# A two-block transformer kernel: the end of the FFN by tile and half, the output stored tile by tile, and the first weight piece of six stages split in halves by ScalarE and VectorE

## The reference

```
for i in range(2):
    h  = modulate_2(rms_norm_2(x, g_norm1[i]), sh1, sc1)
    p  = h @ w_in[i]                       # "proj": 7 column blocks of w_in
    ...                                    # neighbourhood, gating and latent attention
    mix = merge_branches(y_na, y_gm, y_mla, gate_logits, na_w_o, gm_w_o, mla_w_o, w_out)
    x_new = x + gt1 * mix                  # "merge": gates (from h and w_in) times y @ w_o
    x_new = x_new + gt2 * squared_relu_mlp(modulate_2(rms_norm_2(x_new, g_norm2[i]), sh2, sc2),
                                           ffn_w1[i], ffn_w2[i])
return x
```

## Time and profile before

| | us |
|---|---|
| median of 3 runs | 3921.87 |
| lowest and highest of them | 3921.0, 3926.0 |
| time of the profiled execution | 3927.83 |
| its span | 3926.0 |
| TensorE busy in it | 3386.4 (86%) |
| ScalarE, VectorE, GpSimd busy | 1140.5, 1595.3, 648.5 |

### The profile page before, as it was taken

One profiled execution on the slowest core, in us unless ns is written; L12 is line 12 of the kernel. 1 busy time (PEld: TensorE's weight loads), 2 busy tenths in 40 slices (PEclk: granted clock), 3 DMA queues, 4 the chain that ended last, 5 costly groups with the idle time before them and its releaser, 6 DMA issues. The chain is left out here.

```text
span 3926.0 us, 41596 instructions
## 1 busy us (share of the span) xinstructions
PE 3386.4 (86%) x16307; PEld 2397.5 (61%) x16307; DVE 1595.3 (41%) x2658; ACT 1140.5 (29%) x1931; POOL 648.5 (17%) x468
## 2 busy tenths in 40 slices
PE   4999774887756998888999799999599798988998
PEld 2666662222225865456887688888485456867886
DVE  3336642000024635552333533333565553344444
ACT  3113521111123235442221322211235443323221
POOL 2000001000004233123220100000445124400000
PEclk8999786899988989899999899999799999999999
DMA  6883045999976110002112312111611003233332
GB/s 260 330 318 140 2 144 163 429 428 428 428 317 189 61 25 11 9 36 83 65 43 86 118 65 65 55 64 43 200 61 34 9 36 105 86 131 105 97 97 75
DMA packets 162441, 534.02 MB, mean 136 GB/s; under 512 B 12252, under 2 KB 67412, under 8 KB 139228
## 3 DMA queue, kind: packets, MB, share of 16 engines
q1 hardware_dynamic: 139148, 401.22, 27.7%
q0 software_dynamic: 16640, 92.08, 6.7%
q10 hardware_dynamic: 6480, 38.34, 2.5%
HBM read 488.84 MB, written 42.78 MB: 135 GB/s over the span
## 5 line engine op out<-in xcount | busy, mean ns | idle before, releaser
L2926 PE MATMUL ps<-hT_hi,w_hi 128*128 128x512 f32 (+1 forms) x768 | 276.0, 359 | 28.0 <-DVE w_lo L2980 28.0
L2926 PE MATMUL ps<-hT_hi,w_lo 128*128 128x512 f32 (+1 forms) x768 | 275.9, 359 | 0.0
L2926 PE MATMUL ps<-hT_lo,w_hi 128*128 128x512 f32 (+1 forms) x768 | 275.4, 359 | 0.0
L1992 PE MATMUL ps<-wp_hi,hT_hi 128*128 128x512 f32 (+2 forms) x608 | 222.2, 365 | 37.3 <-POOL wp_lo L1971 37.3
L2932 PE MATMUL ps<-w_hi,h_lo 128*128 128x512 f32 x640 | 253.7, 396 | 0.0
L2932 PE MATMUL ps<-w_hi,h_hi 128*128 128x512 f32 x640 | 253.7, 396 | 0.0
L2932 PE MATMUL ps<-w_lo,h_hi 128*128 128x512 f32 x640 | 253.6, 396 | 0.0
L2205 PE MATMUL ps<-Z 64*128 64x256 f32 (+3 forms) x576 | 204.3, 552 | 27.9 <-DVE small L2347 11.6
L2645 POOL TENSOR_TENSOR mr_lo<-ring,wm_hi 128x2048 fp32r<-128x2048 f32 x36 | 171.0, 4763 | 312.8 <-ACT wm_hi L2637 312.7
L1994 PE MATMUL ps<-wp_hi,hm_lo 128*128 128x512 f32 (+2 forms) x608 | 220.0, 362 | 0.0
L2949 ACT ACTIVATE w_hi<-ring 128x2048 fp32r<-128x2048 f32 x64 | 122.0, 1909 | 336.6 <-PE ps L2932 326.8
(11 more groups left out here) (458 smaller groups left out, 6684.6 us busy)
## 6 DMA issues: line engine op xcount, KB each, us to landing
pj<-in_expert_w_up_dram SPq DMA_DIRECT2D x32, 2048.0 KB, 18.3
pj<-in_expert_w_down_dram SPq DMA_DIRECT2D x32, 2048.0 KB, 19.7
ring<-in_expert_w_gate_dram SPq DMA_DIRECT2D x32, 2048.0 KB, 16.0
ring<-in_ffn_w_dram SPq DMA_DIRECT2D x64, 1024.0 KB, 5.2
ring<-in_w_in_dram SPq DMA_DIRECT2D x58, 1024.0 KB, 5.4
Z<-in_w_mod_dram POOLq DMA_DIRECT2D x24, 2048.0 KB, 8.1
Z<-in_w_ada_dram POOLq DMA_DIRECT2D x8, 2048.0 KB, 9.4
ring<-in_w_out_dram SPq DMA_DIRECT2D x12, 1024.0 KB, 10.0
```

Of the source, the lines that this page charges most:

```text
L1992: nc.tensor.matmul(out_, a_hi, b_hi, start=first, stop=False)
L2926: last = nc.tensor.matmul(bank(i % 8, c1 - c0), W[a][:, k, :], r[:, k, c0:c1], start=(k == 0 and r is hhk and a == 0), stop=(k == KT - 1 a ...
```

## The change

**FFN end.** The load of x from `xspill` goes to hT (no longer read then) instead of `xl`, and is issued by ScalarE as soon as the last h-piece is multiplied, that is ahead of y6; the gate load follows it. In y7, VectorE does three operations for each group in place of one: add the bank, multiply by the gate, add x, each on 512 columns with a drain between. In layer 0 the result of tiles 0 to 2 goes straight to `xl`, that of tiles 3 to 5 stays in `yacc` (that part of `xl` is still in use) and is copied after the last group. In layer 1 each finished tile adds to a new semaphore `fin_ok`, on which SP stores that tile (4 DMAs of 0.5 MB).

**First piece.** In proj, merge and FFN of both layers piece 0 is rounded by ScalarE in two halves, and VectorE (in proj and merge instead of GpSimd) makes the two lo halves. TensorE waits for the first half at k = 0 and for the second at the middle k. `w_lo_ok` no longer counts piece 0.

**Merge start.** `unspill` becomes two semaphores. ScalarE rounds the first half of piece 0, waits for the first part of h alone, rounds the first half of hT, then the second half of piece 0. VectorE makes the lo halves ahead of its half of hT. TensorE waits for the first half of `hT_hi` only, and for the second ahead of piece 1.

```
 def round_first(act, hi, w, half):                     # new
     c = slice(w // 2 * half, w // 2 * half + w // 2)
     act.activation(hi[:, c], raw[0][:, c], ACT.Copy).then_inc(first_hi_ok, 1)
 def low_first(dve, stage, l, lo, hi, w, half):         # new
     c = slice(w // 2 * half, w // 2 * half + w // 2)
     dve.wait_ge(first_hi_ok, first_piece(stage, l, half))
     nc.vector.tensor_tensor(lo[:, c], raw[0][:, c], hi[:, c], ALU.subtract).then_inc(first_lo_ok, 1)
...
 # sp_proj
-                if x >= 2:
-                    sp.wait_ge(w_lo_ok, R.fp + x - 1)
+                if x == 2:
+                    sp.wait_ge(first_lo_ok, first_piece("proj", l, 1))
+                if x > 2:
+                    sp.wait_ge(w_lo_ok, R.fp + x - 2)
 # pool_proj, pool_merge
-            for x in range(len(R.pieces)):
+            for x in range(1, len(R.pieces)):
 # pe_proj
-                pe.wait_ge(w_lo_ok, R.fp + x + 1)
+                if x:
+                    pe.wait_ge(w_lo_ok, R.fp + x)
...
+                        if x == 0 and t == ts[0] and k in (0, k1 // 2):
+                            pe.wait_ge(first_lo_ok, first_piece("proj", l, k != 0))
 # act_merge
-            act.wait_ge(unspill, 32 * (l + 1))
+            act.wait_ge(mring_in[0], mring_value(l, 0))
+            round_first(act, wm_hi, 2048, 0)
+            act.wait_ge(unspill[0], 16 * (l + 1))
             act.activation(hT_hi[:, 0:3072], hT[:, 0:3072], ACT.Copy).then_inc(hh_back[0], 1)
-            merge_round(act, p, l, 0, 0)
+            round_first(act, wm_hi, 2048, 1)
 # dve_merge
-            dve.wait_ge(unspill, 32 * (l + 1))
+            for half in range(2):
+                low_first(dve, "merge", l, mr_lo, wm_hi, 2048, half)
+            for s in unspill:
+                dve.wait_ge(s, 16 * (l + 1))
 # act_ffn, after split(x + 2) of each piece; the old end is gone
+                if kind == "h" and hb == FH - 1 and half == 1:
+                    nt = len(TQ[l])
+                    act.wait_ge(mm_done, F.last(x))
+                    act.dma_start(hT[:, 0:nt * D], xspill[:, 0:nt * D]).then_inc(x_back, 16)
+                    act.wait_ge(h1_lo_ok, n["fh"])
+                    load_gate(act, l + 1, 5)
 # dve_ffn, after the add of a y-group
+                        if hb == FH - 1:
+                            if i == groups[0][0] and half == 0:
+                                n["gate"] += 32
+                                dve.wait_ge(gate_in, n["gate"])
+                                dve.wait_ge(x_back, 16 * (2 * l + 2))
+                            c = slice(512 * half, 512 * half + 512)
+                            dve.drain()
+                            nc.vector.tensor_tensor(y, y, gtb[:, what // TL, c], ALU.mult)
+                            dve.drain()
+                            last = nc.vector.tensor_tensor(xl[:, what, c] if l == 0 and what < 3 else y, y, hT[...], ALU.add)
+                            if l == 1 and half == 1:
+                                last.then_inc(fin_ok, 1)
...
+            if l == 0:
+                for t in range(3, TA):
+                    nc.vector.tensor_copy(xl[:, t, :], yacc[:, t, :])
 # end of the program, SP
-            sp.wait_ge(stage_done, F)
-            sp.dma_start(out[0].rearrange("(t p) d -> p t d", p=P), xl[:, 0:TL, :]).then_inc(out_in, 16)
+            for t in LAT:
+                sp.wait_ge(fin_ok, t + 1)
+                sp.dma_start(out[0, P * t:P * t + P, :], yacc[:, t, :]).then_inc(out_in, 16)
```

More of the change, by code:

```diff
@@ L1988, in pe_proj, with first_piece, round_first, low_first @@
                         last.then_inc(half_used, 1)
+        FIRST = {"proj": 0, "merge": 2, "ffn": 4}
+        def first_piece(stage, l, half):
+            return 6 * l + FIRST[stage] + half + 1
+        def round_first(act, hi, w, half):
+            c = slice(w // 2 * half, w // 2 * half + w // 2)
+            act.activation(hi[:, c], raw[0][:, c], ACT.Copy).then_inc(first_hi_ok, 1)
+        def low_first(dve, stage, l, lo, hi, w, half):
+            c = slice(w // 2 * half, w // 2 * half + w // 2)
+            dve.wait_ge(first_hi_ok, first_piece(stage, l, half))
+            nc.vector.tensor_tensor(lo[:, c], raw[0][:, c], hi[:, c], ALU.subtract).then_inc(first_lo_ok, 1)
         def three(out_, a_hi, a_lo, b_hi, b_lo, first, final):
@@ L2036, in dve_project @@
             nt = len(TQ[l])
+            for half in range(2):
+                low_first(dve, "proj", l, WP[0][1], WP[0][0], proj_width(l, Proj(dict(n), l), 0), half)
             dve.wait_ge(prm2, 16 * 7 * (l + 1))
@@ L2641, in pool_merge @@
             merge_counts(n, l)
-            for x in range(18):
+            for x in range(1, 18):
                 n["wr"] += 1
@@ L2654, in half @@
                     kk = 4 * y + k
+                    if j == 0 and y == 0 and t == 0 and k in (0, 2):
+                        pe.wait_ge(first_lo_ok, first_piece("merge", l, k // 2))
                     last = three(bank(b), hhk[:, kk, P * t:P * t + P], hmk[:, kk, P * t:P * t + P],
@@ L2924, in pe_ffn @@
                         for k in range(KT):
+                            if x == 0 and i == groups[0][0] and k in (0, KT // 2):
+                                pe.wait_ge(first_lo_ok, first_piece("ffn", l, k != 0))
                             for a, r in ((0, hhk), (0, hlk), (1, hhk)):
@@ L2949, in split @@
                 act.activation(WHI[x % 2], raw[x % 4], ACT.Copy).then_inc(w_hi_ok, 1)
-            split(0)
+            act.wait_ge(raw_in[0], raw_slot_value(l, 0))
+            for half in range(2):
+                round_first(act, WHI[0], 2048, half)
             split(1)
@@ L2978, in split @@
                     return
[L2979 removed]
+                dve.wait_ge(w_hi_ok, (len(F.pieces) - 1) * l + x)
                 nc.vector.tensor_tensor(WLO[x % 2], raw[x % 4], WHI[x % 2], ALU.subtract).then_inc(w_lo_ok, 1)
[L2982 removed]
+            for half in range(2):
+                low_first(dve, "ffn", l, WLO[0], WHI[0], 2048, half)
             split(1)
@@ L3002, in dve_ffn @@
                             nc.vector.tensor_tensor(y, y, bank(i % 8), ALU.add).then_inc(out_read, 1)
+                        if hb == FH - 1:
[7 more added lines that the diff above has]
+                            dve.drain()
+                            last = nc.vector.tensor_tensor(xl[:, what, c] if l == 0 and what < 3 else y, y, hT[:, D * what + 512 * half:D * what + 512 * half + 512], ALU.add)
+                            if l == 1 and half == 1:
+                                last.then_inc(fin_ok, 1)
                 if kind == "y" and half == 1:
```

60 lines of the change are left out of this document (27 added, 33 removed).

## The result

| | before | after |
|---|---|---|
| median, us | 3921.43 | 3864.95 |
| lowest and highest of four runs | 3919.86, 3926.0 | 3862.29, 3868.79 |
| ratio, 95% interval | | 0.9858, [0.9846, 0.9869] |
| span of the profiled execution | 3926.0 | 3861.0 |

The change takes 56.5 us off, against the 55.5 of the forecast, and 3864.95 lies 1.5 under the forecast time. The two profiled executions differ by more, 65.0: that of before took some 6 us more than its median, that of after 2 less. Of these 65.0, 3.5 are gone ahead of the first changed line: ScalarE begins proj of layer 0 at 1208.55 after and at 1212.02 before.

A forecast was written before the change was run, and what follows sets the result against it. The prediction took TensorE's waits at the starts of proj, merge and FFN, and the serial FFN ends, as the bound. Terms 2.3 + 4.2 + 4.0 + 19.8 + 12.5 + 12.7 = 55.5 us off 3921.87 gave 3866.4, range 3858 to 3880.

The forecast's parts named there:

- proj, layer 0: First weight piece of proj: start 4.2 us earlier, less a new 1.9 us wait at piece 2; gain 2.3 us.
- proj, layer 1: First weight piece of proj: TensorE starts earlier and has 0.8 us to spare at piece 2; gain 4.2 us.
- FFN starts: First weight piece of the FFN in halves: TensorE starts 2.0 us earlier in each layer; gain 4.0 us.
- merge: Merge start: TensorE starts 9.9 us earlier per layer, with no wait at the second half; gain 19.8 us.
- FFN end, layer 0: From the last group's add, three operations and three copies replace a 17.2 us VectorE tail; gain 12.5 us.
- FFN end, layer 1: Final store issued 9.8 us earlier, and 0.5 MB lands in 2.9 us less than 2 MB; gain 12.7 us.
- rival (a): Proj, layer 0: piece 2 follows its earlier release, so the 4.2 us gain is kept; 3864.5 us; chance 0.12.
- Rival (b): Proj: GpSimd gets in ahead of VectorE's second half, costing 4.8 us in layer 1, 2.9 in layer 0; 3874; chance 0.08.
- Rival (e): Merge: TensorE starts only at 1780.8, after VectorE's half of h; 4.1 us less gain per layer; 3875; chance 0.08.
- (c): FFN end: VectorE's two-input operations take 1.33 us, so it falls behind TensorE; 3884 us; chance 0.06.
- (d): FFN end: VectorE falls far behind; operations from 2.2 us eat the whole gain, 4.20 us gives 4010; chance 0.02.

The follow-up runs named there:

- The experiment with both parts: Changed kernel, but ScalarE waits for both parts of h before rounding its first half in merge, as before the change; 3869.26 us.
- both edits: Changed kernel with merge start cut finer and dummy transposes ahead of proj, merge and FFN; 3855.76 us (0.9841), in a longer second series 3856.18 (0.9831).

## Why the prediction was right

Each term, with what the traces give for it. Where two numbers are averaged, the second is from a kernel above that has the same code in that stage.

| term | forecast | measured | from |
|---|---|---|---|
| proj, layer 0 | 2.3 | 2.9 | start 4.17 earlier; TensorE's stretch of proj 203.6 us (mean of seven) after, 202.3 (of two) before |
| proj, layer 1 | 4.2 | 4.4 | start 4.17; stretch 163.4 after, 163.7 before |
| FFN starts | 4.0 | 3.8 | ScalarE's first operation to TensorE's first: 4.45 to 2.53, twice |
| merge | 19.8 | 20.3 | fence to next stage: 330.4 to 320.0, 227.6 to 217.7 (mean of two before, of five after) |
| FFN end, layer 0 | 12.5 | 12.3 | FFN start to next stage: 565.9 to 553.9 and 566.2 to 553.6 |
| FFN end, layer 1 | 12.7 | 14.0 | last matmul to end: 19.2 and 19.5 to 5.4 |
| sum | 55.5 | 57.7 | medians: 56.5 |

**Proj.** The start came out at 2.53 us for the 2.5 forecast. The new wait at piece 2 was sized wrong: 1.9 forecast, 0.49 in the profile after, and 0.4 to 1.5 (mean 1.0) over seven kernels with this proj. Two terms were off. The landing was not unchanged, but about 0.7 us earlier relative to ScalarE's start in this pair: its rounding begins 32.0 us after ScalarE's first operation, 31.7 to 33.0 over the seven, against 32.7 and 35.4 in the two kernels with the old start. So rival (a) is true in part. And pieces 0 and 1 took 35.5 us, not 34.97, since the low clock lasted 4.3 us after TensorE's first matmul and not 3.2 as in before; half of the difference is 0.55. The stretch of before in which it rose (start of TensorE at 1218.72):

```profile
1220.00:1222.00 2.00, 2.00 (x6) 1.52 (x6) 0.00 (x0) 0.00 (x0) 2.00 (x1) 0.52 0.93 389
```

The prediction took over the 34.97 with whatever the clock had done in that one execution. In layer 1 there was room at piece 2, 2.1 us in the mean of the seven kernels, for the 0.8 forecast; one of them waited 0.25. Rival (b) did not come: VectorE's two halves take 2.36 us together, 0.4 ahead of GpSimd's first operation. In the kernel with the whole piece GpSimd began 0.48 us before VectorE had ended: VectorE's operation took 2.29 us as elsewhere, GpSimd's 4.90 in place of 4.57, so the later one paid. No run let GpSimd come first.

**Merge** is the largest term and the best hit: 3.9 us from fence to start, no wait at the second half, a cold clock at 0.50. (In the kernel with the old FFN end the clock fell only as TensorE began; it then stayed low for 3.4 us in each layer.) The experiment with both parts shows that the second part of h is worth a third of it. Rival (e), with its start at the end of VectorE's half of h, is excluded by the rows of both layers.

**FFN end.** Three operations of 0.69 per group, groups 2.81 apart, x there in time: as forecast, with rivals (c) and (d) excluded by their condition, since no operation of y7 took over 0.7 us. In layer 0 the copies took 1.90 us, not 2.25: 0.69 each and partly overlapping, where my nearest row had 0.75. In layer 1 the mis-sized term is the store, 2.6 us where I took 3.7 from a load of the same size; that is most of the 1.3 between 12.7 and 14.0. The Trainium skill ("DMA: Bandwidth & Descriptors", Anatomy of one DMA) gives 3.2 by its formula, which stands there for DMAs that GpSimd issues, while SP issues this one. The row is 0.6 below that, and the row decides.

**How near is near.** The terms sum to 2.2 us more than forecast, and the medians to 1.2 less than the terms; that the forecast time is met to 1.5 us is partly chance. In the profiled pair, besides the 3.5 us ahead of proj, 3.5 us more are gone between proj and merge of layer 0, where nothing was changed. That is no effect of the change: from the end of proj to the first TensorE instruction behind the attention stage's next fence, the same code takes from 182.4 to 188.7 us in the twelve profiled kernels with VectorE's first piece, and 187.1 and 186.6 in the two without. That is a range of 6 us, more than either term of proj or that of the FFN starts, so the terms can only be read from stretches and not from whole times.

## What to carry to other kernels

Where all engines meet at a fence, the time to TensorE's first matmul is a serial chain, and each link of it can be cut: half the work before the first hand-over, the engine with the shortest operation, and a wait only for the part that the first instruction reads. Work behind the last matmul is taken under it by tile, as long as the engine's operations for one group (here a tile and half of the width) stay below TensorE's time for it; beyond that each further operation, 0.77 us with its drain, costs itself once per group. And look which engine issues a DMA: behind a long write in its queue the issue itself may last, and all that the engine has to do next waits with it.

## What the runs showed of the hardware

- A DMA issue behind a 3.8 MB write in the same queue lasted 17.66 us on ScalarE and 18.72 and (for two issues) 22.66 on SP, and held the engine as long. With the write in ScalarE's queue, SP's issue took 0.40.
- Ten transposes of 128 columns took 2.40 us with the clock at 0.50, and fourteen took 1.75 with it at 1.00. Dummy transposes count as work for the clock: the six starts spent 5.4 to 14.4 us at 1.2 GHz with them and 22.8 to 29.3 without. Behind merge's fence the clock did not fall at all with both edits (both layers, both profiles); with the transposes alone it held in layer 1 and fell in layer 0, and without them it fell in both layers of every kernel.
- How long a start stays at 1.2 GHz differs with the same code: at the FFN start of layer 1 it was 3.0 us in one execution and 5.5 in another, at the start of proj of layer 1 2.8 and 5.9. Half of such a difference is in the time of the stage.
- A store of 512 KB landed in 2.6 us, a load of 512 KB in 3.7.
- Three copies of 128 x 1024 f32 within SBUF took 1.90 us together.
